# Two-block model in one kernel: the expert loop written out with gather and scatter inside it, output tiles in pairs, small loads ahead

## The reference, cut to what matters

```
for l in range(2):                       # layer 1: latent stream only behind the attention
    mod = silu(c) @ ada_w[l] + ada_b[l]  # shift, scale, gate of both halves
    y = token_mixers(norm(x) * (1 + sc1) + sh1, ...)   # gating, Fourier, two attentions, w_out
    x = x + g1 * y
    h = norm(x) * (1 + sc2) + sh2
    aff = softmax(h @ router_w[l])       # 16 experts; each takes its best 32 tokens of a stream
    for e in range(16):
        rows = tokens chosen by e
        x[rows] += g2 * aff * ((silu(h[rows] @ w_gate[e]) * (h[rows] @ w_up[e])) @ w_down[e])
```

## Time and profile before

| | |
|---|---|
| median of three runs | 3156.96 us |
| the profiled execution's own time | 3153.11 us |
| its span | 3151.2 us |
| TensorE products, busy | 2928.3 us, 93% |
| VectorE, ScalarE, POOL, busy | 983.1, 550.3, 96.3 us |
| granted TensorE clock, mean | 0.961 |
| HBM read, mean over the span | 667.09 MB, 213 GB/s |
| first product of the expert loop, layer 0 and layer 1 | 467.48 us, 1245.26 us |
| first product of the second block | 1743.43 us |

### The profile page before, as it was taken

The page is one execution under the profiler, slowest core; times in us unless marked ns, Lnnn a source line. Parts: engine busy times, 40 slices in busy tenths (PEclk is TensorE's granted clock), DMA queues, the critical chain, the costliest instruction groups (busy, mean ns, idle before and its releaser), DMA issues.

```text
span 3151.2 us, 32483 instructions
## 1 busy us (share of the span) xinstructions
PE 2928.3 (93%) x12980; PEld 1703.9 (54%) x12980; DVE 983.1 (31%) x1968; ACT 550.3 (17%) x1059; POOL 96.3 (3%) x169
## 2 busy tenths in 40 slices
PE   7999889988889998998998899999999999999998
PEld 3455534333335463433333686674884676674883
DVE  2545432312315453121111344343100434343001
ACT  1143311111111341111010113220000213310000
POOL 2100000000001000000000000001000000000000
PEclk9998889999999998999898999999999999999999
DMA  9413139999997345999999442224344332315342
GB/s 275 142 36 141 54 120 374 409 410 409 410 408 250 112 158 196 397 409 410 409 410 404 129 141 81 81 81 162 134 140 167 134 134 81 107 62 174 139 139 75
DMA packets 237361, 669.79 MB, mean 213 GB/s; under 512 B 8064, under 2 KB 18616, under 8 KB 237248
## 3 DMA queue, kind: packets, MB, share of 16 engines
q1 hardware_dynamic: 230432, 653.28, 55.1%
q0 software_dynamic: 6816, 14.94, 2.1%
HBM read 667.09 MB, written 2.90 MB: 213 GB/s over the span
## 4 chain that ended last, share of the span: by engine, by line
PE 73%; DMA 17%; DVE 5%; ACT 2%; issue 1%; SPq 1%; POOL 1%; DVEq 0%; ACTq 0%; POOLq 0%
PE bank L778 32%; DMA ring<-in_exp_w_up_dram 16%; PE bank L791 10%; PE bank L1342 8%; PE bank L1360 5%; PE bank L1001 3%; PE bank L306 2%; PE bank L1192 2%; PE bank L1137 1%; PE bank L1053 1%; PE bank L933 1%; SPq L511 1%; PE bank L832 1%; PE bank L1163 1%; PE bank L955 1%
## 5 line engine op out<-in xcount | busy, mean ns | idle before, releaser
L791 PE MATMUL bank<-ring,arena 128*64 128x512 f32 (+1 forms) x3072 | 712.6, 620 | 81.3 <-DMA ring<-in_exp_w_up_dram 46.7
L778 PE MATMUL bank<-arena,ring 128*128 128x256 f32 (+1 forms) x2496 | 531.5, 375 | 0.6 <-ACT arena L406 0.6
L791 PEld LDWEIGHTS bank<-ring,arena 128*64 128x64 f32 (+1 forms) x3072 | 215.7, 127 | 555.8 <-issue 477.2
L778 PEld LDWEIGHTS bank<-arena,ring 128*128 128x128 f32 x2496 | 465.3, 191 | 67.1 <-ACT arena L406 1.1
L778 PE MATMUL bank<-ring,arena 128*128 128x512 f32 (+1 forms) x1116 | 470.6, 582 | 3.2 <-DVE arena L2756 2.0
L778 PEld LDWEIGHTS bank<-ring,arena 128*128 128x128 f32 x1116 | 211.6, 191 | 251.9 <-issue 246.9
L1342 PE MATMUL bank<-ring,arena 128*128 128x512 f32 x640 | 295.5, 593 | 0.0
L1360 PEld LDWEIGHTS bank<-ring 128*128 128x128 f32 x1248 | 154.0, 192 | 42.0 <-issue 37.3
L2445 DVE COPY arena<-bank 128x512 f32<-128x512 f32 (+1 forms) x64 | 44.0, 688 | 424.5 <-PE bank L791 424.5
L306 PE MATMUL bank<-arena 128*128 128x128 f32 (+5 forms) x608 | 87.8, 291 | 86.2 <-DVE arena L2273 17.2
L1342 PEld LDWEIGHTS bank<-ring,arena 128*128 128x128 f32 x640 | 112.0, 191 | 92.8 <-issue 92.8
(11 more groups left out here) (298 smaller groups left out, 2286.8 us busy)
## 6 DMA issues: line engine op xcount, KB each, us to landing
ring<-in_exp_w_gate_dram SPq DMA_DIRECT2D x64, 2048.0 KB, 23.6
ring<-in_exp_w_up_dram SPq DMA_DIRECT2D x64, 2048.0 KB, 23.8
ring<-in_exp_w_down_dram SPq DMA_DIRECT2D x64, 2048.0 KB, 20.3
ring<-in_w_in_dram SPq DMA_DIRECT2D x42, 2048.0 KB, 7.7
ring<-in_ada_w_dram SPq DMA_DIRECT2D x24, 2048.0 KB, 12.3
ring<-in_w_ffn_up_dram SPq DMA_DIRECT2D x20, 2048.0 KB, 7.8
ring<-in_w_out_dram SPq DMA_DIRECT2D x8, 2048.0 KB, 10.0
ring<-in_w_ffn_down_dram SPq DMA_DIRECT2D x8, 2048.0 KB, 7.7
```

Of the source, the lines that this page charges most:

```text
L778: last = mm(o, lhs(k), rhs(k), start=start and k == 0, stop=stop and k == kt - 1)
L791: last = mm(U(us[c])[g * rows:(g + 1) * rows, :], lhs(k), rhs(i, c), start=(k < 2), stop=(k >= KT - 2))
```

## The change

- The hardware loop over expert groups is written out. `gather` before it selects for the first group only, 16 products of 128 columns for a stream; the next group's tokens are gathered in experts 1 and 2 of a group, and the results of the group before are returned in two halves, in experts 0 and 3 (`between`). In the first group there is nothing to return, and its expert 3 transposes the weighted selections. POOL's copies are gone; TensorE reads the gathered tokens where they were put.
- In layer 1, where an expert has 32 rows, the gate and up products go into four partition groups instead of two.
- Layer 1's beginning (transpose and first modulation product, and VectorE's work on them) is put ahead of the last return of layer 0.
- In layer 0 the output tiles run as two pairs, the steps of one tile in turn with those of the other, and `fill_table` is spread anew: the first pair starts at entry 37 instead of 31 and three entries have no step, so that the second pair comes wholly behind the attention.
- Nine of the 15 small loads stand ahead of layer 1's loop; the other six have their own semaphore, `gates2`, which is waited for after the first four units of products.
- `keep_busy` also stands ahead of the attention and in `route`.

Its core (VectorE's and ScalarE's programs follow the same order; `added` takes one half tile at a time):

```
 PRE_CHUNKS = 19
-LAYER_USES = PRE_CHUNKS + 1 + 6 * N_EXP
+LAYER_USES = PRE_CHUNKS + 6 * N_EXP
+GROUPS = N_EXP // 4
...
         def streams(l):
             return range(2) if l < DEPTH - 1 else range(1)
+
+        def between(l, g, e):
+
+            ns = len(streams(l))
+            if e in (1, 2) and g < GROUPS - 1:
+                return [("gather", i) for i in range((e - 1) * ns, e * ns)]
+            if g == 0:
+                return [("turn", t) for t in tiles(l)] if e == 3 else []
+            halves = {0: 0, (1 if g == GROUPS - 1 else 3): 1}
+            if e in halves:
+                return [("scatter", t, c) for t in tiles(l)[halves[e] * ns:(halves[e] + 1) * ns] for c in range(2)]
+            return []
+
...
             rest = [1] * (entries - until)
             if l == DEPTH - 1:
                 rest[-2] = 0
+            else:
+                for i in (9, 18, 27):
+                    rest[i] = 0
             return table + rest
+
+        def output(l, out_tile):
+
+            if l == DEPTH - 1:
+                for t in tiles(l):
+                    yield from out_tile(t)
+                return
+            for t in (0, 2):
+                other = out_tile(t + 1)
+                for step in out_tile(t):
+                    yield
+                    next(other, None)
+                    yield
+                next(other, None)
 
         def in_turn(*programs):
...
                 q = count[0]
-                nc.sync.wait_ge(sem["chunk_used"], LAYER_USES * l + PRE_CHUNKS - RING + q + (1 if q < RING else 2))
+                nc.sync.wait_ge(sem["chunk_used"], LAYER_USES * l + PRE_CHUNKS - RING + q + 1)
                 s = EXPERT_SLOTS[l][q % RING]
                 count[0] += 1
...
-                            eng.tensor_copy(
-                                GROUP_SEL[:, 0:ns, :],
-                                m["gate"].rearrange("p (s n) -> p s n", s=2)
-                                [:, 0:ns, bass.ds(g * SEQ, SEQ)]).then_inc(sem["group_in"], 1)
-                            nc.gpsimd.wait_ge(sem["group_in"], gp.due("group_in"))
+                if l == DEPTH - 1:
+                    get(CAUSAL, A["c_causal_t"], "smalls2")
+                    get(PICK[:, 0:15], A["c_pick"], "smalls2")
+                    get_rows_2(0)
                 nc.gpsimd.wait_ge(sem["moe_done"], gp.due("moe_done"))
                 if l < DEPTH - 1:
                     get_first(l + 1)
                     get_lam_and_router(l + 1)
                     get(SEQDFT, A["c_seq_dft"].rearrange("(k p) n -> p k n", p=P), "smalls")
             for l in range(DEPTH):
-
+                if l:
+                    get_rows_2(l)
                 if l == 0:
...
-                    get(STRICT, A["c_strict_t"], "smalls2")
-                    get(m2["levels"], A["c_levels"], "smalls2")
-                    get(PICK[:, 0:15], A["c_pick"], "smalls2")
-                get(m2["rows"][0:96, :], A["conv_w_2"][l].rearrange("i (t p) -> (i t) p", p=P), "smalls2")
-                get(m2["rows"][96:104, :], A["g_mlstm_norm_2"][l].rearrange("(k p) -> k p", p=P), "smalls2")
-                get(m2["rows"][104:105, :], A["g_gdn_norm_2"][l:l + 1, :], "smalls2")
+                    get(STRICT, A["c_strict_t"], "gates2")
+                    get(m2["levels"], A["c_levels"], "gates2")
                 for at, first, n in ((0, W2_BETA, 8), (32, W2_I, 4), (64, W2_F, 4), (96, W2_A, 8)):
-                    get(WG[:, :, at:at + n], A["w_in_2"][l, :, first:first + n].rearrange("(k p) n -> p k n", p=P), "smalls2")
-                for at, i, name, n in ((32, 0, "b_igate_2", 4), (64, 0, "b_fgate_2", 4), (96, 2, "dt_bias_2", 8), (0, 3, "a_log_2", 8)):
-                    get(VEC[at:at + n, i:i + 1], A[name][l].rearrange("(n a) -> n a", a=1), "smalls2")
+                    get(WG[:, :, at:at + n], A["w_in_2"][l, :, first:first + n].rearrange("(k p) n -> p k n", p=P), "gates2")
                 nc.gpsimd.wait_ge(sem["heads_done"], gp.due("heads_done"))
...
+            def begin(l):
+
+                nc.tensor.wait_ge(sem["rows_in"], pe.due("rows_in", 16 * (9 if l == 0 else 7)))
+                chunks[0] = 0
+                u = bank_for()
+                turn(U(u)[:, 0:92], ROWS[0:92, :]).then_inc(full[u % BANKS], 1)
+                if l == 0:
+                    nc.tensor.wait_ge(sem["silu_c"], pe.due("silu_c"))
+                for step in modulation(l, 0):
+                    pass
+
+            begin(0)
...
+                    spare = keep_busy(BUSY_PRODUCTS, DENSE)
                     nc.tensor.wait_ge(sem["xn_ready"], pe.due("xn_ready"))
                     turned = []
                     for j in range(2):
@@ -1098,8 +1118,7 @@
                         if j > 6:
                             ada_fold(j - 1, DENSE)
                     ada_fold(9, DENSE)
-                    for t in tiles(l):
-                        yield from out_tile(t)
+                    yield from output(l, out_tile)
 
                 def last_ada():
 
@@ -1121,8 +1140,8 @@
                     yield
...
-                    for k in range(KT):
+                    for i in range(2):
                         u = bank_for(RULE)
-                        for t in range(2):
-                            last = mm(U(u)[:, :].rearrange("p (b n) -> p b n", b=4), XN[:, 2 * s + t, k * P:(k + 1) * P],
-                                      sel(2 * s + t), start=(t == 0), stop=(t == 1))
+                        for j in range(4):
+                            k = 4 * i + j
+                            for t in range(2):
+                                last = mm(U(u)[:, j * P:(j + 1) * P], XN[:, 2 * s + t, k * P:(k + 1) * P],
+                                          sel(2 * s + t)[:, 0, :], start=(t == 0), stop=(t == 1))
...
+                def gather_next(g, i):
+
+                    u = bank_for()
+                    for j, (k, s) in enumerate(gather_items(l, i)):
+                        for t in range(2):
+                            last = mm(U(u)[:, j * P:(j + 1) * P], XN[:, 2 * s + t, k * P:(k + 1) * P],
+                                      sel(2 * s + t)[:, g, :], start=(t == 0), stop=(t == 1))
+                    last.then_inc(full[u % BANKS], 1)
+                    return u
+
+                def turn_weighted(t):
+
+                    nc.tensor.wait_ge(sem["selg_ready"], pe.due("selg_ready"))
+                    u = bank_for()
+                    for b in range(4):
+                        last = turn(U(u)[:, b * P:(b + 1) * P], SELW[:, t, b, :])
+                    last.then_inc(full[u % BANKS], 1)
+                    return u
...
                 assert held[0] == 0
-                held[0] = 1
                 M = 32 * ns
-                with pe.loop(4, expert_turn(ns)) as g:
+                turned, down_units = [], []
+                for g in range(GROUPS):
                     for e in range(4):
-                        nc.tensor.wait_ge(sem["xgc_ready"], pe.due("xgc_ready"))
+                        if e == 0:
+                            evacuated(gathered_units)
+                            gathered_units = []
                         ups, halves = [], []
                         for w_i in range(2):
-                            us = [pe.unit(), pe.unit()]
-                            for u in us:
-                                nc.tensor.wait_ge(free[u % BANKS], pe.uses(u - BANKS))
+                            us = [bank_for(), bank_for()]
                             for half in range(2):
                                 w = wide[next_chunk(EXPERT_SLOTS[l])]
-                                halved(us, M, lambda k: XGC[:, e % 2, k, 0:M], lambda i, c: w[:, i, c * CN:(c + 1) * CN], half)
+                                halved(us, M, lambda k: XG[g % 2][:, k, e, 0:M], lambda i, c: w[:, i, c * CN:(c + 1) * CN],
+                                       half, P // M)
...
                                 for i in range(4):
                                     last = mm(U(u)[:, (4 * j + i) * M:(4 * j + i + 1) * M],
-                                              parts[0:2 * M, c, i * P:(i + 1) * P], FOLD[M], start=True, stop=True)
-                                    if c == 0 and i == 0 and j == 0:
-                                        last.then_inc(sem["xg_used"], 1)
-                                    if c == 0 and i == 1 and j == 0:
+                                              parts[:, c, i * P:(i + 1) * P], FOLD[M], start=True, stop=True)
+                                    if held[0]:
                                         release(last)
...
-                        if e == 0:
-                            scatter(D * nt // 8)
-                        for n_out in halves:
-                            nc.tensor.wait_ge(free[n_out % BANKS], pe.uses(n_out))
-                        us = [pe.unit(), pe.unit()]
-                        for u in us:
-                            nc.tensor.wait_ge(free[u % BANKS], pe.uses(u - BANKS))
```

(25 more changed lines are left out.)

372 lines of the change are left out of this document (170 added, 202 removed).

## The result

| | before | after |
|---|---|---|
| median of the runs | 3157.22 us (3151.11 to 3159.38, 4 runs) | 3099.51 us (3094.55 to 3109.47, 4 runs) |
| profiled execution, its span | 3153.11 us, 3151.2 us | 3100.39 us, 3098.4 us |

The ratio is 0.9819, its 95% interval 0.9802 to 0.9836: 57.7 us or 1.8% less. The predicted 3075 was 24.5 us too low. The outer range 3048 to 3108 holds the time, the forecast's own range of 3055 to 3094 does not. The changed kernel was timed once more beside later experiments: 3100.71 us, ratio 0.9827 (0.9814 to 0.9841).

A forecast was written before the change was run, and what follows sets the result against it. Expert loops were taken as bound by weight transfer at 410 GB/s, the rest by TensorE with idle time and lowered clock. Terms summed to 80.8 us, giving 3072.3 to 3076.2, stated as 3075; own range 3055 to 3094, outer 3048 to 3108.

The forecast's parts named there:

- outer range: Whole kernel: 3048 to 3108 us, leaving out the slower rival and the tails.
- output tiles in pairs: Layer 0's output stage: fewer waits and 12 us of clock regained, gain 22 us, bounds 5 and 33.
- gather, layer 0: Before layer 0's expert loop: gathering one group shortens 37.7 us to 10.9, gain 26.8, bounds 23 and 28.
- first turn, layer 0: Layer 0's first expert: nothing to return, so no transfer stall and an earlier first slot, gain 4.2 us.
- start of layer 1: Layer boundary: turn and modulation product moved into TensorE's wait, last transposes ready 2.8 us sooner, bounds 0 and 5.
- gather, layer 1: Before layer 1's expert loop: 19.9 us becomes 7.3, gain 12.6, bounds 10 and 14.
- first turn and end, layer 1: Layer 1's loop: first turn gains 3.5 us with four partition groups; the end loses 0.5 through a lower clock.
- small loads: Start of the second block: the 9.40 us wait for late loads goes, gain 9.4 us, bounds 7 and 11.
- The sign of being wrong that was named: Layer 0's output stage: one stated sign of error was its keeping 46 us of waits and lost clock.
- pairing gives nothing: Layer 0's output tiles: VectorE runs the chains serially with routing mixed in, gain 2 instead of 22, 3095 us; chance 0.15.
- the slower rival: Layer 1's loop: TensorE starves to the lower clock and becomes the bound, 3237 us; chance 0.05.
- the moved work inside the loops: Expert loops: moved gather and return products make an expert 28.7 us, under the transfer's 30.7, so cost nothing.

The follow-up runs named there:

- e8: Changed kernel, but layer 0's fourth output tile takes PSUM banks 6 and 7 instead of sharing the third's two: 3094.65 us, ratio 0.9799.
- e5: Changed kernel with the next layer's first turn and first modulation product behind the last scatter products again: 3104.26 us, ratio 0.9837.
- yardstick: The changed kernel again, unedited, timed on the same chip as e5, e6 and e7: 3100.71 us, ratio 0.9827.
- e3: Changed kernel, layer 0's output tiles one after the other except tile 2's last four steps in turn with tile 3's first four: 3104.28 us, ratio 0.9836.
- e4: Changed kernel with all 15 small loads issued after the last expert again and waited for before the second block's first transposes: 3115.09 us, ratio 0.9863.
- e6: Changed kernel with layer 1's gate and up products in two partition groups instead of four: 3100.85 us, ratio 0.983.
- e7: Changed kernel with the gather products inside both expert loops made twice: 3101.11 us, ratio 0.9829.
- e2: Changed kernel without identity products for the second tile of a pair and the routing step in layer 0: 3100.19 us, ratio 0.9814.
- e11: As e10, with layer 1's gate and up products in two partition groups: 3095.2 us, ratio 0.9786.
- e10: As e8, plus 12 identity products in the 2.35 us wait ahead of layer 0's expert loop: 3090.56 us, ratio 0.9777.

## Why the prediction was right and where it was wrong

The measured terms are differences of marks in the two profiled executions, whose spans lie 52.8 us apart.

| step | predicted | measured | from |
|---|---|---|---|
| output tiles in pairs | 22 | 1.7 | gather at 429.81, 428.13 |
| gather, layer 0 | 26.8 | 26.0 | 37.7, 11.7 us |
| first turn, layer 0 | 4.2 | 3.4 | loop 468.4 (to a last fold at 935.88), 465.0 us |
| start of layer 1 | 2.8 | -2.4 | last fold to projection 42.5, 44.9 us |
| layer 1 up to its gather | 0 | -1.8 | 247.0, 248.8 us |
| gather, layer 1 | 12.6 | 11.4 | 19.9, 8.5 us |
| first turn and end, layer 1 | 3.5 - 0.5 | 0.6 | loop 464.9, 464.3 us |
| small loads | 9.4 | 11.4 | 33.2, 21.8 us |
| second block | 0 | 2.6 | 1407.8, 1405.2 us |
| sum | 80.8 | 52.9 | |

The measured sum is 27.9 us short of the predicted one, and 20.3 of that is the first row.

*The step that failed is the pairs' term.* It was said that "with two tiles in turn, the other tile's products stand in the last two" waits (gain 10.5), that the chain's wait grows to about 9 with a sum of 12.5, and that 12 us of clock come back. The longest wait was well sized, 8.0 us, but with the wrong cause: it is a wait for a bank, which I had not looked for. Two tiles in turn need two banks each, and their lane has two. The waits for data did shrink, from 24.3 to 7.4 us, and 11.4 us of waits for a bank took their place. And a term was put at nothing without a reason: inside the attention VectorE makes the second tile's chain ahead of the attention's own step, and TensorE waits 6.4 us there where it had waited 0.6. So idle time is 33.6 us before and 33.2 after. The clock's loss, busy x (1 - clock), over all windows up to the gather is 24.1 us before (22.3 up to 417 us, and 8.00 us busy at 0.77 behind it) and 18.8 after, so 5.3 back and not 12. Of these more work took 4.0: busy x clock up to the gather grew from 239.1 to 243.1 us, as 36 more identity products stand there, ahead of the attention and in `route`. The sign of being wrong that was named, an output stage that keeps its 46 us of waits and lost clock, is what is seen: 25.2 + 18.8 = 44.0 us. The rival "pairing gives nothing", at 3095, described what came, with the right order of events (VectorE serial, routing mixed in) and without the bank; the outer range held because this rival lay in it. e8 shows the missing part by giving it: idle time of 24.7 us, clock loss 16.1 from its windows, the gather 14.5 us earlier than before. The new wait in the first pair stays there, 5.9 us. Even then 22 would not have been reached, and a third of the 12.4 us won over the changed kernel was lost again in the loop, about half of that behind its slow first products.

Windows of e8 over the same stage, cut in the same way (attention's end 338.2, output products 362.3 to 390.0, gather 415.3):

```profile
133.00:250.00 117.00, 112.80 (x570) 0.99 0.30 101
250.00:300.00 50.00, 42.08 (x218) 0.86 0.46 168
300.00:338.20 38.20, 34.75 (x181) 0.96 0.00 1
338.20:362.30 24.10, 16.55 (x106) 0.78 0.47 174
362.30:390.00 27.70, 27.70 (x68) 1.00 0.21 76
390.00:415.30 25.30, 23.74 (x176) 0.83 0.44 167
```

*Start of layer 1:* the early start is worth what was said (e5: 2.8 us), the sign of the sum was not. With the down products at the full clock the seam is 42.1 us in the yardstick, and 41.3 to 46.1 in the other executions of the same instructions there (e3 and e4 the longest, 45.7 and 46.1); before it was 42.5. So even at the full clock nothing is seen of the gain. In the yardstick the loss lies behind the scatter: from the last fold to the scatter it is 14.8 us, before 14.9 (950.83 - 935.88). There TensorE waits 2.36 us for modulation weights, which before it did not; in e3 and e4 it waits 2.6 and 3.0 us for them. The forecast had only TensorE's and VectorE's work in this seam and no transfer. Why the weights come late, and what the new order of VectorE's copies adds, was not tried.

*First turn, layer 1:* 3.5 was mis-sized: with the end of the loop 0.6 us came instead of 3.0, and 2.1 in the yardstick. It rested on layer 0's stall and on a shorter last up chunk. The last up chunk took 3.64 us in four groups, the time of the lower clock, where two groups had taken 3.63 at the full one; e6 finds two groups no slower.

The Trainium skill ("TensorE: Matmul & The Clock Gate", section "HAM oscillation — how this bites in real kernels") has the rule that bursts waiting for the next transfer are put back to half rate. The trace agrees for this chunk, 3.64 instead of 1.92 us; the loop did not pay for it, as its traffic stayed at 409 GB/s and the 3237 us of the slower rival did not come.

*Right within a microsecond or so:* both gathers, layer 0's first turn, nothing for the moved work inside the loops (e7 doubles the gather part). *Small loads:* 11.4 us and, in the first eight products, 2.1 more (9.25 to 7.10), which is why the second block shows 2.6; the upper bound 11 had a part of it. e4 gives 13.3 in its profile (33.1 - 21.8, and 9.16 - 7.10).

The 1.8 us that layer 1's attention stage seems to lose are the spread of executions: in the yardstick, the same program, the stretch is 246.6 us, and in the experiments it lies between 246.5 and 251.1. Why the clock at the layer boundary is low in one execution and not in the next stays open.

## What to carry to other kernels

When two instances of a stage are to run in turn, count the buffers that each holds at once before counting waits: with too few, the second waits for the first's buffer under the name of the engine that empties it, and here neither another order (e3) nor less work ahead of it (e2) helped. Count too what the second instance's chain delays on an engine that other work needs: here the attention's step, by 6.0 us. Read such a wait by what the waiting instruction needs; a constant operand means that it waits for its output. And where a transfer sets a loop's pace, what is won ahead of the loop is partly lost again if the first users of the buffers are slow.

## What the runs showed of the hardware

The loop's first 32 products took 15.48 to 15.64 us where the gather ahead of them had taken 9.63 to 9.90 us, and 13.95 where it had taken 8.77 to 9.48 (eleven executions with an idle gap of 2.35 us between the two). With twelve identity products, 2.84 us, in the gap they took 13.96 us behind a gather of 9.90 (e11) and 13.95 behind one of 8.94 (e10), and the 48 after the fold 20.82 us, where e8 has 22.48. One profile of e11 is what shows the filling at work. In layer 1's loop the granted clock fell from 0.90 to 0.80 to 0.88 with four partition groups and rose to 0.95 with two, at the same traffic.

The same instructions up to the attention's end took between 338.0 and 345.9 us in six executions (the changed kernel twice, e4 to e7), with clocks of 1.00 to 0.90 in the first 133 us. A mark of one profile is good to a few microseconds; the stretch behind the attention held within 0.6 us (87.9 to 88.5). That is why the experiments were read by stretches. Not every stretch is as steady: the seam of the two layers took 41.3 to 46.1 us, and layer 0's loop 465.0 to 469.3.
